# An encoder layer with 32 experts: from pair 8 on, gate/up weights are requested two experts less far ahead, behind the down weights of the next pair

## What is computed

```python
comb = (one_hot(expert_id, 32) * weight[..., None]).sum(1)      # two experts per token
out = zeros((256, 1024))
for e in range(32):
    hg, hu = split(t @ w_gate_up[e], 2, axis=-1)                # w_gate_up[e]: 1024 x 512
    out = out + comb[:, e:e + 1] * ((silu(hg) * hu) @ w_down[e])  # w_down[e]: 256 x 1024
return layer_norm(alpha * x + out, ln2_g, ln2_b)
```

## Time and profile before

| what | value |
|---|---|
| median of 3 runs | 495.59 us (495.35 to 497.16) |
| the profiled execution, its own time | 495.22 us |
| its span, first to last instruction | 493.0 us |
| TensorE matmul busy | 470.1 us, 95% of the span |
| VectorE, GpSimd, ScalarE busy | 245.6, 223.2, 202.4 us |
| chain that ended last | TensorE 86%, VectorE 5%, ScalarE 3%, issue 2% |
| the loads' queue (q1) | 144.67 MB, 74.7% of 16 engines' span |
| mean granted TensorE clock | 0.986 of full speed |

### The profile page before, as it was taken

One profiled execution on the slowest core, in us unless ns is written; L12 is line 12 of the kernel. 1 busy time (PEld: TensorE's weight loads), 2 busy tenths in 40 slices (PEclk: granted clock), 3 DMA queues, 4 the chain that ended last, 5 costly groups with the idle time before them and its releaser, 6 DMA issues.

```text
span 493.0 us, 7686 instructions
## 1 busy us (share of the span) xinstructions
PE 470.1 (95%) x2816; PEld 333.0 (68%) x2816; DVE 245.6 (50%) x536; ACT 202.4 (41%) x447; POOL 223.2 (45%) x187
## 2 busy tenths in 40 slices
PE   7999999999999999999998999999999999889992
PEld 6999999898999999988973544444444434334431
DVE  1089999759996445640689242222222222122116
ACT  3544554498875696554542242221221211122112
POOL 3899899766865778999308021111111110011002
PEclk9999999999999999999998999999999999989997
DMA  8799988523533445549938999999999999999702
GB/s 289 255 362 367 362 296 329 196 104 120 181 128 129 130 170 169 175 172 364 423 150 320 361 368 427 422 418 423 420 421 421 423 419 421 422 420 422 292 0 86
DMA packets 26370, 145.13 MB, mean 294 GB/s; under 512 B 3040, under 2 KB 3296, under 8 KB 13792
## 3 DMA queue, kind: packets, MB, share of 16 engines
q1 hardware_dynamic: 26336, 144.67, 74.7%
HBM read 143.61 MB, written 1.05 MB: 293 GB/s over the span
## 4 chain that ended last, share of the span: by engine, by line
PE 86%; DVE 5%; ACT 3%; issue 2%; DMA 2%; SPq 1%; POOL 1%; DVEq 0%; ACTq 0%
PE bank L1493 21%; PE bank L1245 12%; PE bank L1528 12%; PE bank L1247 12%; PE bank L1246 12%; PE bank L1543 3%; PE bank L1544 3%; DMA raw<-in_w_in 2%; PE bank L1323 1%; PE bank L1301 1%; PE bank L1517 1%; DVE info L1132 1%; POOL w_lo L497 1%; PE bank L1467 1%; PE bank L1468 1%
## 5 line engine op out<-in xcount | busy, mean ns | idle before, releaser
L497 POOL TENSOR_TENSOR w_lo<-raw,w_hi 128x512 fp32r<-128x512 f32 x140 | 183.1, 1326 | 46.9 <-ACT w_hi L562 43.6
L562 ACT CAST w_hi<-raw 128x512 fp32r<-128x512 f32 x140 | 85.2, 620 | 80.5 <-PE bank L1247 75.6
L1245 PE MATMUL bank<-x_hi,w_hi 128*128 128x256 f32 x400 | 115.5, 289 | 1.4 <-POOL w_lo L497 1.4
L1247 PE MATMUL bank<-x_hi,w_lo 128*128 128x256 f32 x400 | 113.2, 283 | 0.0
L1246 PE MATMUL bank<-x_lo,w_hi 128*128 128x256 f32 x400 | 113.1, 283 | 0.0
L523 POOL COPY raw<-gates 128x512 f32 x28 | 19.8, 706 | 161.0 <-PE bank L1493 140.9
L808 DVE SCALAR_TENSOR_TENSOR bank<-slots,par,bank 128x256 f32<-128x256 f32 x232 | 92.3, 481 | 0.2
L1493 PE MATMUL bank<-slots,raw 128*64 128x512 f32 x320 | 84.5, 592 | 0.0
L1245 PEld LDWEIGHTS bank<-x_hi,w_hi 128*128 128x128 f32 x400 | 76.6, 192 | 2.1 <-issue 1.3
L1246 PEld LDWEIGHTS bank<-x_lo,w_hi 128*128 128x128 f32 x400 | 76.7, 192 | 0.3
L1247 PEld LDWEIGHTS bank<-x_hi,w_lo 128*128 128x128 f32 x400 | 76.7, 192 | 0.0
(11 more groups left out here) (213 smaller groups left out, 655.8 us busy)
## 6 DMA issues: line engine op xcount, KB each, us to landing
slots<-in_w_gate_up SPq DMA_DIRECT2D x40, 1024.0 KB, 13.5
slots<-in_w_down SPq DMA_DIRECT2D x32, 1024.0 KB, 15.9
raw<-in_w_in SPq DMA_DIRECT2D x48, 512.0 KB, 4.2
extra<-in_w_gate_up SPq DMA_DIRECT2D x8, 1024.0 KB, 12.0
spare<-in_w_gate_up SPq DMA_DIRECT2D x8, 1024.0 KB, 16.0
late<-in_w_gate_up SPq DMA_DIRECT2D x8, 1024.0 KB, 18.7
raw<-in_w_attn SPq DMA_DIRECT2D x8, 512.0 KB, 3.3
raw<-in_w_conv SPq DMA_DIRECT2D x8, 512.0 KB, 3.3
```

Source lines behind the costliest of these rows:

```text
L497: nc.gpsimd.tensor_tensor(w_lo[:, n % SPLIT, m], raw[:, b % RAW, m], w_hi[:, n % SPLIT, m].bitcast(F32), ALU.subtract).then_inc(w_lo_done, 1)
L562: nc.scalar.copy(w_hi[:, n % SPLIT, m], raw[:, b % RAW, m]).then_inc(w_hi_done, 1)
L1245: mm(dst, ah, bh, start=first, stop=False, **kw)
L1247: return mm(dst, al, bh, start=False, stop=last, **kw)
```

## The change

`refilled_to(p)` says up to which expert gate/up weights have been requested once step p of the loop is over. Up to p = 7 nothing moves (2p + 7 is the old limit). From p = 8 on the limit is 2p + 5. Step 8 therefore requests no gate/up weights, and each later step requests those of 2p + 3 and 2p + 4. Steps 14 and 15 request expert 31 and none; before, steps 13 and 14 did. The same 96 transfers are made, into the same homes. The line numbers of the new file are 7 higher from here on.

```diff
-FIRST_REFILL = 6
+FAR_AHEAD_TO = 8
...
+def refilled_to(p):
+
+    if p < SLOTS // 2:
+        return 10
+    return min(EXPERTS, 2 * p + (7 if p < FAR_AHEAD_TO else 5))
...
                 if p == SLOTS // 2:
                     refill((8, 9))
-                    refill((10,))
-                else:
-                    refill([e for e in (2 * p + 5, 2 * p + 6) if e < EXPERTS])
+                refill(range(refilled_to(p - 1), refilled_to(p)))
```

## The result

| | before | the change |
|---|---|---|
| median | 495.88 us (4 runs, 495.35 to 497.16) | **488.76 us** (4 runs, 486.77 to 489.20) |
| ratio, with its 95% interval | | 0.9853 (0.9826 to 0.9880) |
| profiled execution, its span | 495.22, 493.0 us | 486.77, 484.6 us |
| mean granted TensorE clock | 0.986 | 0.992 |

The change makes the kernel 7.1 us, 1.5%, faster. Forecast were 489.0 us, with a range of 488.0 to 491.0.

What follows compares the result with a forecast made beforehand. It took a full load pipe in the wrong order, making TensorE wait for down weights, as the bound. Savings of 4.62 + 1.77 + 0.21 = 6.6 us from 495.22 gave 488.6, plus 0.37 for the median: 489.0 us, range 488.0 to 491.0.

Steps and rivals of the forecast that it cites:

- What bounds it: Pairs 10 to 13: TensorE waits for down weights queued behind gate/up weights used two pairs later, 4.6 us in sum.
- Does the pipe stay full?: At step 9: its request comes 5.8 us before the queue's work ends, so transfers keep landing every 2.484 us.
- The lead into an empty queue: Load queue: a request into an empty queue lands after 4.9 us, 2.48 of them the transfer, leaving 2.4 us.
- The landings against the needs: Pairs 10 to 15: every listed load lands before a never-pausing TensorE needs it; smallest margin 1.6 us, at down(14).
- The sum, 6.6 us: Pairs 10 to 15: waits 4.62, slow block 1.77 and three other down blocks 0.21 us are all saved.
- the slow `down(12)`: Pair 12: the block took 5.35 us instead of 3.58 at a reduced clock; this 1.77 us loss goes with the waits.
- the four waits: TensorE's waits for down weights ahead of down(10) to down(13), 0.56, 1.91, 1.90 and 0.25 us; all 4.62 us go.
- The clock as a rival: Pairs 10 to 15: TensorE still gets 1.2 GHz for a stretch, costing 1.8 us, 490.8 us; chance 0.07.
- The moved wait: Gate/up matmuls: the loads set the pace, so 6.6 us of waits move there from down, 495.6 us; chance 0.04.
- the dry queue: Steps 9 to 15: an empty queue costs 2.4 us per step, 504.2 us with all seven; chance 0.02.
- The slower pipe: Load transfers: at 362 GB/s each takes 2.90 us, giving 499.4 us; chance 0.01.
- The span: Whole profiled execution in the new profile: expected to be 486.4 us.

Runs made afterwards that it cites:

- e5: Changed kernel, but each step after 8 requests its gate/up refills ahead of its down weights, restoring the old queue order at the change's distance; 495.59 us, ratio 0.9988.
- e6: Changed kernel with gate/up weights requested one expert less far ahead from step 8 on, instead of two; 491.91 us, ratio 0.9891.
- e7: Changed kernel with the switch to the shorter request distance at step 4 instead of 8; 491.99 us, ratio 0.9890.
- e4: Changed kernel with gate/up weights requested four experts less far ahead from step 8 on, instead of two; 496.85 us, ratio 1.0024.
- e1: Changed kernel with the switch to the shorter request distance at step 12 instead of 8; 494.36 us, ratio 0.9969.
- e3: Kernel before the change, with throwaway matmuls filling TensorE's pauses before down(10) to down(13); 494.90 us, ratio 0.9997.
- e9: Changed kernel with three throwaway matmuls in TensorE's one pause ahead of pair 0; 487.13 us, ratio 0.9836.
- e2: e1 with throwaway matmuls filling TensorE's pauses before down(10) to down(12); 492.90 us, ratio 0.9951.

## Why the prediction was right, and where it was not

- **What bounds it.** Right: a full pipe whose order was wrong. e5 shows that it is the order, e6 that half the shift leaves half of the lateness (3.3 us of 6.5).
- **Does the pipe stay full?** Right: it carries on at 2.49 us per transfer through step 9, which came 6.2 us before the queue was empty (foreseen 5.8). The condition behind it, work in the queue when the next step comes, is real: e7 and e4 break it and pay. The lead into an empty queue, 2.4 us, held both times (4.8 and 4.9 us to landing).
- **The landings against the needs.** Right to within 0.4 us: a margin of 1.2 us at `down(14)` for the 1.6 foreseen. The landings themselves came 1.4 us earlier than in my list (375.5 for 376.9), with TensorE 1.8 us earlier for the most part because of `down(0)`. I had not foreseen that a single transfer can slip by 1.4 us (e4), or that the loads of one execution run 1.1 us later than those of another (e1). In this execution no transfer slipped; a slip of 1.4 us would have used up the margin of 1.2.
- **The sum, 6.6 us.** D fell by 6.55 us. That it fits so closely says only that TensorE no longer waits, since D before is the one that I had worked from; that the medians lie 7.1 us apart and the forecast is off by 0.2 us is in part luck, as D before varies by 1.5 us. The total is right, **one of its terms is not what I took it for**. I counted the slow `down(12)` as 1.77 us that are lost beside the four waits, "zero if the clock falls anyway". e3 shows that in the kernel before this stretch was free: with the full clock, `down(13)` waits those 1.7 us longer for the same landing. The 6.55 us are the lateness of `down(13)`, which started with its weights at 451.57 us instead of 445.08, 6.49 us, and 0.07 us for that block at 3.65 us. The waits and the slow block merely share this time out. Adding both up gave the right number, because between the last landing that is waited for and the last undisturbed start all time lost is lateness, whatever its name in the chain.
- **The clock as a rival** was priced rightly for a kernel in which nothing is late behind it (e1, e6: 1.8 us in full), and did not occur in pairs 9 to 15 of the changed kernel, in the two profiles taken of it and in that of e9.
- **The moved wait, the dry queue.** Both exist, the dry queue in e4 and e7, the waits at `gate_up` in e4 and in part in e7, and neither at the distance and the step chosen. The slower pipe was not seen: 419 to 422 GB/s in the full windows.
- **The span.** It was 484.6 us and not 486.4, because of `down(0)`.

## What to carry to other kernels

When loads wait for each other in one full queue, write the landing time of every transfer (order times the price of one) beside the time at which it is needed by an engine that never waits; the order is good when the margins are all positive, and the largest negative one is what can be won. Waits and slow blocks between two late landings must not be added up as if each could be won by itself. Requesting something later is safe only as long as the queue still holds work when the next request is allowed; a hole made there is paid for where the margin is smallest, even 100 us later.

## What the runs showed of the hardware

- **Behind some pauses of 1.90 to 2.04 us a `down` ran partly at the lower clock, behind others not.** In the profiles of the kernel before, e1, e5 and e6 one `down` took 5.35 us, behind a pause of 1.90, 1.90, 2.02 and 2.04 us; a pair earlier there had been one of 1.91, 1.90, 1.94 and 1.26 us, and the block behind that took 3.65 us. A second pause is not enough either: in e1 the earlier one of 1.90 us was itself the second, a pair after one of 1.55 us, and in e7 no block was slow behind 0.59, 1.38 and 1.36 us. What decides it is not shown. In the kernel before, the slow `down(12)` started at full clock, at 436.63 us, and lost it about 1.3 us later (the number before the last two of each row is the granted clock):

```profile
437.00:438.00 1.00, 1.00 (x7) 0.38 (x5) 0.00 (x0) 0.00 (x0) 0.00 (x0) 0.96 1.00 418
438.00:440.50 2.50, 2.50 (x8) 0.88 (x6) 0.69 (x1) 0.58 (x1) 0.00 (x0) 0.50 1.01 419
```

The Trainium skill ("TensorE: Matmul & The Clock Gate", HAM oscillation) says that waits for DMA between bursts of matmuls can put the clock back to its lower level, so that the next burst starts slow. The runs agree that such waits do it, with pauses that were filled (e2, e3) as the counterproof; that the burst starts slow is not what this row shows, where the clock fell inside it.
- **Throwaway matmuls kept the clock up.** Eight instructions in 1.83 us, inside a pause of about 1.9 us, were enough in the profiles of e2 and e3. The 12 executions of e3 have a mean clock of 0.989 to 0.995, the 32 of the kernel before beside them 0.985 to 0.992.
- **The pipe is very even, with rare slips.** 36 transfers of 1 MB ran at 2.48 us each in the kernel before. A single slip of 1.4 us (e4) stayed in the later landings.
- **A block right behind a pause costs 0.07 us more** (3.65 for 3.58), at full clock, with the pause filled or not.
